# Experts of a routed layer: row gathers that skip empty slots, and finished rows written by GpSimd scatters

## The chip, the core and the metric

The kernel runs on one core of a Trainium2 chip. The core has five engines with queues of their own: TensorE (PE; its weight loads stand as PEld), VectorE (DVE), ScalarE (ACT), GpSimd (POOL) and SyncE (SP), and 16 DMA engines that serve all queues. The metric is the device time of one execution in microseconds, as a median of runs.

## The reference

Two blocks of a transformer on 512 tokens of width 1024. What matters is the mixture of experts at the end of the first block: 32 experts, each token goes to 4.

```
logits = hf @ router_w + router_b
top_val, top_idx = lax.top_k(logits, TOP_K)            # TOP_K = 4, 512 tokens
gate = softmax(top_val)
...
def expert_block(args):
    e, toks, wts = args
    u = hf[toks] @ w1[e] + b1[e]                       # w1[e]: 1024 x 2048
    g_, lin = u[:, :D_FF], u[:, D_FF:]
    g_ = jnp.minimum(g_, SWIGLU_LIMIT)
    lin = jnp.clip(lin, -SWIGLU_LIMIT, SWIGLU_LIMIT)
    y = ((lin + 1.0) * g_ * sigmoid(SWIGLU_ALPHA * g_)) @ w2[e] + b2[e]
    return y * wts[:, None]
...
out = segment_sum(y.reshape(R, D), row_tok, num_segments=T)
```

Everything is float32. The attention of two kinds ahead of the experts, and the second block behind them, are not touched but for one transfer.

## The kernel before

**Stages.** The program goes through stages with a barrier of all engines between them: norm and projections, attention (`attention`, to about 387 us of the profile), output projection and routing (`output_and_route`, to 480), the experts (`expert_blocks`, to 1554), `combine_and_norm`, and the second block.

**Blocks.** Each expert's tokens are the rows of one block; the row's slot in the block is its rank among the expert's tokens, so a block's real rows are its first ones. Experts are sorted by their count and laid out so that even blocks (and block 31) hold up to 128 rows and the other odd blocks up to 64: 17 blocks of 128 slots and 15 of 64. Rows past that go to overflow blocks (up to 15, blocks 32 to 46), which run only if there are any; in this profile there are none. A slot that has no row names token 0.

**Row traffic.** `output_and_route` writes the normed tokens to the DRAM tensor `h_dram` (h_rows in the profile) and builds `slots`, a token number for each slot of each block. In the experts GpSimd copies a block's column of `slots` into `col` (L1745) and gathers the rows of `h_dram` into `xg` by an indirect DMA (L1748), 128 or 64 rows of 4 KB. `xg` is single, so `next_rows(b)` waits until PE has transposed the block before (`x_turn`). A finished block is moved by ACT from PSUM into the SBUF tile `y` (L2030 for 128 rows, L2022 for 64) and stored by ACT's own DMA queue into `y_dram` (y_rows) as one contiguous piece (L2032, L2024); the next copy into `y` waits for `stored`. `combine_and_norm` gathers four rows of `y_dram` for each token.

**Weights.** Each expert has 12 chunks of 1024 KB. SP loads them into a ring of 8 slots (L1228) when PE has used a slot, ACT rounds a chunk into `w_hi` (L1997), DVE makes the rest `w_lo` by a subtraction (L2149), and PE multiplies with both. ACT's order is written by hand in `to_small(i)` and `from_small(i)`: 12 roundings, with the moves of rows in between. In `to_small` the odd block's `y` is copied after the fifth rounding (`few_rows_out`) and the even block's after the twelfth (`rows_out`).

**Zeros.** So that no row of `y_dram` that is never written holds garbage, the attention's SP fills the 15 overflow blocks with zeros (L932, last in SP's list for that stage), and `output_and_route` copies rows of x into the unused upper 64 slots of the odd blocks (L1306).

## Time and profile before

| | us |
|---|---|
| median of 3 runs | 3497.16 (3491.63 to 3498.02) |
| the profiled execution | 3498.6 |
| its span, first to last instruction | 3496.5 |
| experts, first chunk of the stage to the last store | about 480 to 1554 |

The page shows what each engine did over the whole span and in 40 slices of 87.4 us each. The experts fill slices 6 to 18. Shares of the whole span are means over stages with different limits; for this change the stage's own windows and waits are to be read.

### The profile page before, as it was taken

To read this page: it belongs to the slowest core of one execution; us is meant where nothing else is said; L and a number is where in the kernel's file an instruction comes from. 1 tells how busy PE (TensorE), PEld (TensorE's weight loads), DVE (VectorE), ACT (ScalarE), POOL (GpSimd) and SP (SyncE) were. 2 spreads that over 40 slices of the span, in tenths; PEclk is the share of its full clock that TensorE was granted. 3 is DMA by queue.
4 is the path that set the end of the run, shared out by engine and by line. 5 is a ranking of instruction groups with operands and counts; after the bars stand their busy time and mean duration, and the time that the engine had idled before them with its cause. 6 is when DMAs were issued, how large, how long until landed. Compare 5 with 4: busy or idle time off the path is not lost. (4 is left out here: it accounts for less than half of the span.)

```text
span 3496.5 us, 38713 instructions
## 1 busy us (share of the span) xinstructions
PE 3183.6 (91%) x13402; PEld 2163.4 (62%) x13402; DVE 2868.0 (82%) x4755; ACT 1432.8 (41%) x1763; POOL 714.8 (20%) x724
## 2 busy tenths in 40 slices
PE   7999989999999999999999999888888888888876
PEld 5878767777777777766788788543444434344422
DVE  6867689999999999967995645788888788888886
ACT  3235448888888888853233632111111111111110
POOL 0000001000000000010000200344444444444443
PEclk9999999999999999999999999999999999999999
DMA  7422279999999999974234025999999999999998
GB/s 264 168 85 103 75 261 393 407 407 403 406 405 401 406 403 403 410 273 138 95 98 133 13 97 199 391 421 417 421 412 415 413 407 421 418 417 410 414 421 344
DMA packets 251798, 1100.57 MB, mean 315 GB/s; under 512 B 21208, under 2 KB 30832, under 8 KB 185840
## 3 DMA queue, kind: packets, MB, share of 16 engines
q1 hardware_dynamic: 166221, 523.62, 39.3%
q0 software_dynamic: 79680, 558.14, 39.0%
q10 hardware_dynamic: 5760, 17.04, 1.2%
q8 instruction: 78, 1.28, 0.1%
q14 instruction: 59, 0.48, 0.0%
HBM read 1069.64 MB, written 33.03 MB: 315 GB/s over the span
## 5 line engine op out<-in xcount | busy, mean ns | idle before, releaser
L2149 DVE TENSOR_TENSOR moe_w_lo<-ring,moe_w_hi 128x2048 fp32r<-128x2048 f32 x384 | 860.7, 2282 | 27.9 <-ACT moe_w_hi L1997 26.5
L1997 ACT ACTIVATE moe_w_hi<-ring 128x2048 fp32r<-128x2048 f32 x380 | 721.6, 1916 | 163.7 <-DMA ring<-in_exp_w 149.0
L2938 PE MATMUL last_banks<-last_rows_b,ring 128*128 128x512 f32 x1024 | 504.4, 640 | 126.0 <-DVE ring L3138 125.8
L2938 PE MATMUL last_banks<-last_rows_a,ring 128*128 128x512 f32 x1024 | 476.7, 609 | 85.3 <-DVE ring L3138 84.9
L3030 ACT ACTIVATE last_gelu<-last_dot 128x2 f32<-128x2 f32 (+1 forms) x257 | 52.3, 203 | 1116.1 <-DVE last_dot L3135 1116.0
L2938 PEld LDWEIGHTS last_banks<-last_rows_b,ring 128*128 128x128 f32 x1024 | 198.8, 203 | 405.6 <-issue 211.2
L2938 PEld LDWEIGHTS last_banks<-last_rows_a,ring 128*128 128x128 f32 x1024 | 188.5, 193 | 327.8 <-issue 198.4
L2817 POOL DMA_INDIRECT last_rows_a<-in_peer_uv,last_ids x256 | 282.3, 1103 | 507.3 <-PE last_banks L2938 329.8
L2817 POOL DMA_INDIRECT last_rows_b<-in_peer_uv,last_ids x256 | 290.4, 1134 | 383.6 <-PE last_banks L2938 363.5
L3138 DVE TENSOR_SCALAR ring<-consts_sb,last_gelu,last_gates 128x128 f32<-128x128 f32 x512 | 162.0, 387 | 78.7 <-ACT last_gelu L3030 77.8
L1745 POOL COPY moe_col<-slots 128x1 uint32 (+1 forms) x30 | 35.7, 1191 | 861.3 <-PE moe_tp L1793 477.0
L3135 DVE CUSTOM_DVE_ANT_0 last_rows_b<-last_rows_b,ring 128x1024 f32<-128x1024 f32 x128 | 155.3, 1224 | 50.0 <-DMA last_rows_b<-in_peer_uv,last_ids 47.5
L3135 DVE CUSTOM_DVE_ANT_0 last_rows_b<-last_rows_b,last_h 128x1024 f32<-128x1024 f32 x128 | 154.5, 1223 | 37.0 <-DMA last_rows_b<-in_peer_uv,last_ids 34.0
L3135 DVE CUSTOM_DVE_ANT_0 last_rows_a<-last_rows_a,ring 128x1024 f32<-128x1024 f32 x128 | 154.0, 1221 | 35.8 <-DMA last_rows_a<-in_peer_uv,last_ids 34.7
L3135 DVE CUSTOM_DVE_ANT_0 last_rows_a<-last_rows_a,last_h 128x1024 f32<-128x1024 f32 x128 | 153.4, 1221 | 30.0 <-DMA last_rows_a<-in_peer_uv,last_ids 28.6
L2565 DVE SCALAR_TENSOR_TENSOR conv_rows<-glu,conv_taps,conv_rows 128x512 f32<-128x512 f32 x240 | 160.8, 741 | 0.5
L260 DVE TENSOR_TENSOR mix_lo<-ring,mix_hi 128x2048 fp32r<-128x2048 f32 (+1 forms) x48 | 107.2, 2245 | 49.4 <-ACT mix_hi L251 49.1
L251 ACT ACTIVATE mix_hi<-ring 128x2048 fp32r<-128x2048 f32 (+1 forms) x48 | 90.0, 1882 | 116.9 <-DMA ring<-in_w_in 50.9
L307 PE MATMUL conv_acc<-mix_hi,ht_hi 128*128 128x512 f32 x320 | 126.3, 395 | 0.0
L309 PE MATMUL conv_acc<-mix_hi,ht_lo 128*128 128x512 f32 x320 | 125.6, 393 | 0.0
L308 PE MATMUL conv_acc<-mix_lo,ht_hi 128*128 128x512 f32 x320 | 124.9, 390 | 0.0
L1083 DVE COPY spare<-att_pt 128x128 f32<-128x128 f32 (+3 forms) x160 | 78.2, 489 | 44.4 <-PE att_pt L975 40.8
(599 smaller groups left out, 6345.9 us busy)
## 6 DMA issues: line engine op xcount, KB each, us to landing
ring<-in_exp_w SPq DMA_DIRECT2D x384, 1024.0 KB, 11.5
ring<-in_w_in SPq DMA_DIRECT2D x38, 1024.0 KB, 5.4
ring<-in_ada_w SPq DMA_DIRECT2D x12, 1024.0 KB, 13.1
z<-in_ada_w SPq DMA_DIRECT2D x12, 1024.0 KB, 7.2
y_rows<-moe_y ACTq DMA_DIRECT2D x17, 512.0 KB, 6.7
ring<-in_w_out SPq DMA_DIRECT2D x8, 1024.0 KB, 5.0
y_rows<-spare SPq DMA_DIRECT2D x1, 7680.0 KB, 25.2
gate_rows<-conv_held ACTq DMA_DIRECT2D x4, 1024.0 KB, 8.2
```

What stands on the lines that cost most here:

```text
L251: self.env.nc.scalar.activation(self.hi[:, m % RAW, 0:n], self.raw[:, i % RAW, 0:n], ACT.Copy).then_inc(self.hi_done, 1)
L260: self.env.nc.vector.tensor_tensor(self.lo[:, i % RAW, 0:n], self.raw[:, i % RAW, 0:n], self.hi[:, m % RAW, 0:n].bitcast(F32), ALU.subtrac ...
L307: nc.tensor.matmul(out, lhs[0], rhs[0], start=start, stop=False)
L308: nc.tensor.matmul(out, lhs[0], rhs[1], start=False, stop=False)
L309: return nc.tensor.matmul(out, lhs[1], rhs[0], start=False, stop=stop)
L1997: nc.scalar.activation(w_hi[:, slot, :], env.ring[:, slot, :], ACT.Copy).then_inc(hi_done, 1)
L2149: nc.vector.tensor_tensor(w_lo[:, slot, :], env.ring[:, slot, :], w_hi[:, slot, :].bitcast(F32), ALU.subtract).then_inc(lo_done, 1)
L2565: ins = nc.vector.scalar_tensor_tensor(conv[:, n, :], glu[:, n, tap:tap + S], taps[:, n, tap:tap + 1], conv[:, n, :], ALU.mult, ALU.add)
L2817: nc.gpsimd.indirect_dma_start(slot(n), None, d["peer_uv"], bass.IndirectOffsetOnAxis(ids[:, u % 4, s:s + 1], 0)).then_inc(gathered[n % SL ...
L2938: last = nc.tensor.matmul(sums(t)[:, q, :], diag[:, n % SL], slot(n)[:, D + q * W:D + (q + 1) * W], start=first, stop=final)
L3135: nc.vector.tensor_tensor_reduce(left, left, h(t), 1.0, 0.0, ALU.mult, ALU.add, dot[:, n % SL:n % SL + 1]).then_inc(dotted, 1)
L3138: nc.vector.tensor_scalar(diag[:, n % SL], ident, act_out[:, n % SL:n % SL + 1], gates[:, u % 4, n % K:n % K + 1], ALU.mult, ALU.mult).the ...
```

## The change

Four things change.

- `slots` of an empty slot becomes a number past the end (`NO_ROW`), and the gathers get a bounds check that leaves such rows out. To tell an empty slot, the routing's count by block and slot uses t + 1 in place of t for the four token tiles, so that zero means empty.
- A second table `out_at` holds, for each block and slot, the row of `y_dram` to write, or `NO_ROW`. GpSimd copies its column into `out_col` and scatters `y` into `y_dram` by an indirect DMA with a bounds check. ACT's DMA issues and their waits are gone; ACT still copies PSUM into `y`, and still waits for `stored` before the next copy.
- GpSimd's order in the experts becomes gather, scatter, gather, scatter: `next_rows(b)` is followed by `rows_out(b - 3)`.
- `y_dram` is zeroed as a whole (47 blocks and not 15) in the attention, and the copies of x into unused slots go away.

```diff
-    attention(env, "att1", (z, z, z), heads, fill=y_dram[N_EXP * P:], ...)
+    attention(env, "att1", (z, z, z), heads, fill=y_dram, ...)
...
-            unused = m["y_dram"][0:N_EXP * P, :].rearrange("(g f r) n -> f g r n", f=4, r=HALF)[3]
-            some_rows = d["x"].rearrange("(g r) n -> g r n", r=HALF)
-            for g0, g1 in ((0, 8), (8, N_EXP // 2 - 1)):
-                sp.dma_start(unused[g0:g1], some_rows[0:g1 - g0]).then_inc(filled, 16)
...
-            sp.wait_ge(filled, 32)
...
-                chain.also(nc.vector.tensor_scalar(own, own, float(t), None, ALU.mult))
+                chain.also(nc.vector.tensor_scalar(own, own, float(t + 1), None, ALU.mult))
...
-            chain(nc.vector.tensor_copy(rows_lo[:], rows_ps[:, 0:NB]))
+            chain(nc.vector.tensor_scalar(empty[:], rows_ps[:, NB:2 * NB], 0.5, NO_ROW, ALU.is_lt, ALU.mult))
+            chain(nc.vector.tensor_scalar(rows_lo[:], iota[:, 0:NB], float(P), env.const("tok")[:, 0:1], ALU.mult, ALU.add))
+            chain(nc.vector.tensor_tensor(m["out_at"][:], rows_lo[:], empty[:], ALU.add))
+            chain(nc.vector.scalar_tensor_tensor(rows_lo[:], rows_ps[:, 0:NB], -float(P), empty[:], ALU.add, ALU.add))
             chain(nc.vector.scalar_tensor_tensor(m["slots"][:], rows_ps[:, NB:2 * NB], float(P), rows_lo[:], ALU.mult, ALU.add))
 
+NO_ROW = float(MAX_BLOCKS * P + 2 * S)
...
-                nc.gpsimd.indirect_dma_start(xg[0:rows], None, h_dram, bass.IndirectOffsetOnAxis(col[0:rows, 0:1], 0)).then_inc(gathered, 16)
+                nc.gpsimd.indirect_dma_start(xg[0:rows], None, h_dram, bass.IndirectOffsetOnAxis(col[0:rows, 0:1], 0),
+                                               bounds_check=S - 1, oob_is_err=False).then_inc(gathered, 16)
+
+            def rows_out(b, rows=P):
+                pool.wait_ge(y_moved, b + 2)
+                pool.sem_inc(tick, 1)
+                nc.gpsimd.tensor_copy(out_col[:], out_at[:, span(b, 1)]).then_inc(out_ready, 1)
+                pool.wait_ge(out_ready, b + 1)
+                pool.sem_inc(tick, 1)
+                nc.gpsimd.indirect_dma_start(y_dram, bass.IndirectOffsetOnAxis(out_col[0:rows, 0:1], 0), y[0:rows], None,
+                                             bounds_check=MAX_BLOCKS * P - 1, oob_is_err=False).then_inc(stored, 16)
...
-            with pool.Fori(0, (N_EXP - 4) // 2) as i2:
-                next_rows(i2 * 2 + 2, P)
-                next_rows(i2 * 2 + 3, HALF)
+            next_rows(2, P)
+            next_rows(3, HALF)
+            rows_out(0)
+            with pool.Fori(0, (N_EXP - 6) // 2) as i2:
+                next_rows(i2 * 2 + 4, P)
+                rows_out(i2 * 2 + 1, HALF)
+                next_rows(i2 * 2 + 5, HALF)
+                rows_out(i2 * 2 + 2)
             next_rows(N_EXP - 2, P)
+            rows_out(N_EXP - 5, HALF)
             next_rows(N_EXP - 1, P)
+            rows_out(N_EXP - 4)
+            rows_out(N_EXP - 3, HALF)
+            rows_out(N_EXP - 2)
+            rows_out(N_EXP - 1)
...
             def few_rows_out(b, n_small):
                 act.wait_ge(y_done, n_small + 1)
                 nc.scalar.activation(y[0:HALF], flat(yp, HALF), ACT.Copy).then_inc(y_moved, 1)
-                act.wait_ge(y_moved, b + 2)
-                act.dma_start(y_dram[span(b * P, HALF), :], y[0:HALF]).then_inc(stored, 16)
...
             def rows_out(b, chunks):
                 act.wait_ge(used, chunks)
-                act.wait_ge(stored, b * 16 + 16)
+                if not isinstance(b, int) or b > 0:
+                    act.wait_ge(stored, b * 16)
                 nc.scalar.activation(y[:], yp[:].rearrange("p q n -> p (q n)"), ACT.Copy).then_inc(y_moved, 1)
-                act.wait_ge(y_moved, b + 2)
-                act.dma_start(y_dram[span(b * P, P), :], y[:]).then_inc(stored, 16)
```

On GpSimd, the loop over pairs of blocks in the experts, before (moe_col is `col`, moe_xg the gathered rows, h_rows the tokens in DRAM):

```order
L1745 COPY moe_col<-slots 128x1
L1746 REGISTER_ALU
L1748 DMA moe_xg<-h_rows,moe_col 128x1024
L1751 REGISTER_ALU
L1753 REGISTER_ALU
L1745 ISA
L1745 COPY moe_col<-slots 128x1
L1746 REGISTER_ALU
L1748 DMA moe_xg<-h_rows,moe_col 64x1024
```

and now (moe_y is the finished block's tile, moe_out_col the column of rows to write, y_rows the target in DRAM):

```order
L1748 DMA moe_xg<-h_rows,moe_col 128x1024
L1753 REGISTER_ALU
L1755 ISA
L1755 COPY moe_out_col<-out_at 128x1
L1756 REGISTER_ALU
L1758 DMA y_rows<-moe_y,moe_out_col 6016x1024
L1762 REGISTER_ALU
L1764 REGISTER_ALU
L1745 ISA
L1745 COPY moe_col<-slots 128x1
L1746 REGISTER_ALU
L1748 DMA moe_xg<-h_rows,moe_col 64x1024
```

A scatter of the odd block now stands between the two gathers, and one of the even block behind the second.

On ACT, the end of the same loop from the copy of the odd block's rows, before:

```order
L2022 ACTIVATE moe_y<-moe_yp 64x1024
L2024 ISA
L2024 DMA y_rows<-moe_y 64x1024
L1997 ACTIVATE moe_w_hi<-ring 128x2048 x2
...
L2030 ACTIVATE moe_y<-moe_yp 128x1024
L2032 ISA
L2032 DMA y_rows<-moe_y 128x1024
```

and now:

```order
L2045 ACTIVATE moe_y<-moe_yp 64x1024
L2020 ACTIVATE moe_w_hi<-ring 128x2048 x2
...
L2051 REGISTER_ALU
L2052 ACTIVATE moe_y<-moe_yp 128x1024
```

The two DMA issues have left ACT's queue; the copies stand where they stood.

## Rows read from the trace of the kernel before

**Rows 1.** The page: busy time by engine, and DMA share in 40 slices.

```profile
PE 3183.6 (91%) x13402; PEld 2163.4 (62%) x13402; DVE 2868.0 (82%) x4755; ACT 1432.8 (41%) x1763; POOL 714.8 (20%) x724
...
DMA  7422279999999999974234025999999999999998
```

**Rows 2.** Windows: stretch, busy us of each engine, granted clock, DMA share, GB/s.

```profile
600.00:1400.00 800.00, 766.15 (x3461) 593.41 (x3460) 777.26 (x461) 656.78 (x446) 64.75 (x48) 1.00 1.03 405
```

**Rows 3.** Waits from 600 to 1400: us in total, times, longest.

```profile
ACT moe_w_hi L1997 <- DMA ring<-in_exp_w: 121.3, 153, 2.0
...
DVE moe_w_lo L2149 <- ACT moe_w_hi L1997: 20.9, 28, 1.5
```

**Rows 4.** Timeline of ACT: start, duration, instruction, idle time before it.

```profile
815.53 1.91 ACT L1997 ACTIVATE moe_w_hi<-ring 128x2048 fp32r<-128x2048 f32 x1 [0.65 <-DMA ring<-in_exp_w]
818.09 1.91 ACT L1997 ACTIVATE moe_w_hi<-ring 128x2048 fp32r<-128x2048 f32 x1 [0.65 <-DMA ring<-in_exp_w]
...
830.89 1.92 ACT L1997 ACTIVATE moe_w_hi<-ring 128x2048 fp32r<-128x2048 f32 x1 [0.63 <-DMA ring<-in_exp_w]
834.73 1.92 ACT L1997 ACTIVATE moe_w_hi<-ring 128x2048 fp32r<-128x2048 f32 x1 [1.92 <-DMA ring<-in_exp_w]
```

**Rows 5.** Windows: a 128-row gather lands (first), 64-row gathers land (others).

```profile
831.00:834.00 3.00, 3.00 (x14) 2.45 (x13) 3.00 (x2) 1.80 (x1) 0.00 (x0) 1.00 1.02 408
860.00:863.00 3.00, 3.00 (x15) 2.43 (x14) 3.00 (x2) 1.83 (x2) 0.00 (x0) 1.00 1.03 296
926.00:929.00 3.00, 3.00 (x15) 2.44 (x14) 3.00 (x2) 2.49 (x2) 0.00 (x0) 1.00 1.03 306
793.00:796.00 3.00, 3.00 (x14) 2.44 (x13) 3.00 (x3) 2.47 (x3) 0.00 (x0) 1.00 1.04 328
```

**Rows 6.** Window: the store of 128 rows is under way.

```profile
869.00:872.00 3.00, 2.79 (x13) 1.96 (x12) 3.00 (x2) 1.38 (x2) 0.00 (x0) 1.00 1.03 423
```

**Rows 7.** Timeline of GpSimd.

```profile
523.59 4.62 POOL L1745 COPY moe_col<-slots 128x1 uint32 x1 [25.41 <-PE moe_tp L1785]
...
824.06 1.91 POOL L1745 COPY moe_col<-slots 128x1 uint32 x1 [33.37 <-PE moe_tp L1793]
826.76 0.97 POOL L1748 DMA_INDIRECT moe_xg<-h_rows,moe_col  x1 [0.79 <-POOL moe_col L1745]
...
853.38 0.22 POOL L1745 COPY moe_col<-slots 128x1 uint32 x1 [25.65 <-PE moe_tp L1785]
854.39 2.29 POOL L1748 DMA_INDIRECT moe_xg<-h_rows,moe_col  x1 [0.78 <-POOL moe_col L1745]
...
890.29 1.91 POOL L1745 COPY moe_col<-slots 128x1 uint32 x1 [33.61 <-PE moe_tp L1793]
```

**Rows 8.** Timeline of ACT: copies of finished rows into y.

```profile
845.31 1.01 ACT L2022 ACTIVATE moe_y<-moe_yp 64x1024 f32<-64x1024 f32 x1
...
863.82 1.01 ACT L2030 ACTIVATE moe_y<-moe_yp 128x1024 f32<-128x1024 f32 x1
```

**Rows 9.** The page, DMA issues: KB each, median us from issue to landing.

```profile
ring<-in_exp_w SPq DMA_DIRECT2D x384, 1024.0 KB, 11.5
...
y_rows<-moe_y ACTq DMA_DIRECT2D x15, 256.0 KB, 5.9
```

**Rows 10.** Timeline of DVE: the router's last instruction.

```profile
478.39 0.21 DVE L1650 SCALAR_TENSOR_TENSOR slots<-out_acc,out_rows_lo 128x47 uint32<-128x47 f32 x1
```

**Rows 11.** Timeline of ACT and of GpSimd: the last store, the first combining gather.

```profile
1551.74 0.35 ACTq L2032 DMA_DIRECT2D y_rows<-moe_y  x1
...
1556.16 1.07 POOL L2296 DMA_INDIRECT got_rows<-y_rows,dest  x1 [104.04 <-POOLq L189]
```

**Rows 12.** Timeline of SP, and SP's wait for the zeros.

```profile
271.03 1.12 SPq L932 DMA_DIRECT2D y_rows<-spare  x1
386.92 0.38 SPq L1298 DMA_DIRECT2D z<-in_ln_g  x1
...
SPq L892 <- DMA y_rows<-spare: 24.1, 1, 24.1
```

More of the change, by code:

```diff
@@ L1177, in dve_between @@
             pieces.split_part(dve, splits.index(g) % 4)
-    attention(env, "att1", (z, z, z), heads, fill=y_dram[N_EXP * P:], loads=loads, act_between=act_between, dve_between=dve_between)
+    attention(env, "att1", (z, z, z), heads, fill=y_dram, loads=loads, act_between=act_between, dve_between=dve_between)
 def first_mixer(env, mod, y_dram, blocks):
@@ L1271, in output_and_route @@
         destf = sb("destf", [P, N]); blk = sb("blk", [P, N], U32); slot = sb("slot", [P, N], U32)
-        blkf = sb("blkf", [P, N]); slotf = sb("slotf", [P, N]); rows_lo = sb("rows_lo", [P, NB])
+        blkf = sb("blkf", [P, N]); slotf = sb("slotf", [P, N]); rows_lo = sb("rows_lo", [P, NB]); empty = sb("empty", [P, NB])
         acc = ps("acc", [P, 4, W])
@@ L1284, in output_and_route @@
             "eps_set", "copied", "chain"))
-        lifted, filled, first_ok, first_rows, compared, ordered, at_ok, at_done, numbered, x_turn, x_hi, row_names = (sem(n) for n in (
-            "lifted", "filled", "first_ok", "first_rows", "compared", "ordered", "at_ok", "at_done", "numbered", "x_turn", "x_hi", "row_names"))
+        lifted, first_ok, first_rows, compared, ordered, at_ok, at_done, numbered, x_turn, x_hi, row_names = (sem(n) for n in (
+            "lifted", "first_ok", "first_rows", "compared", "ordered", "at_ok", "at_done", "numbered", "x_turn", "x_hi", "row_names"))
         first_xg, first_col = gather_place(nc, "out1", m["rows_at"])
@@ L1657, in gather_place, with expert_blocks @@
     return nc.alloc_sbuf_tensor_at(f"{name}_xg", [P, D], F32, offset=at), nc.alloc_sbuf_tensor_at(f"{name}_col", [P, 1], U32, offset=at + 4 * D)
-def expert_blocks(env, slots, expert_at, over_expert, n_over, row_pick, parts, h_dram, y_dram, landed, rows_at, col_ready, gathered, hi_done, lo_done, w_hi, w_lo, bend, first_x_lo, first_xt):
+def expert_blocks(env, slots, out_at, expert_at, over_expert, n_over, row_pick, parts, h_dram, y_dram, landed, rows_at, col_ready, gathered, hi_done, lo_done, w_hi, w_lo, bend, first_x_lo, first_xt):
     nc, d = env.nc, env.d
@@ L1775, in _ @@
                     gather(o + N_EXP)
+                    rows_out(o + N_EXP)
             pool.sem_inc(tick, 1)
@@ L2022, in few_rows_out @@
                 nc.scalar.activation(y[0:HALF], flat(yp, HALF), ACT.Copy).then_inc(y_moved, 1)
-                act.wait_ge(y_moved, b + 2)
-                act.dma_start(y_dram[span(b * P, HALF), :], y[0:HALF]).then_inc(stored, 16)
             def rows_out(b, chunks):
                 act.wait_ge(used, chunks)
-                act.wait_ge(stored, b * 16 + 16)
+                if not isinstance(b, int) or b > 0:
+                    act.wait_ge(stored, b * 16)
                 nc.scalar.activation(y[:], yp[:].rearrange("p q n -> p (q n)"), ACT.Copy).then_inc(y_moved, 1)
-                act.wait_ge(y_moved, b + 2)
-                act.dma_start(y_dram[span(b * P, P), :], y[:]).then_inc(stored, 16)
             def to_small(i, eights, n_small, first=False):
@@ L2087, in _ @@
             act.sem_inc(y_moved, 1)
-            act.sem_inc(stored, 16)
             act.sem_inc(x_hi, 2)
@@ L2116, in _ @@
                     rows_out(b, o * 12 + MAIN_CHUNKS + 12)
-            act.wait_ge(stored, n * (16 * MAX_OVER) + (N_EXP + 1) * 16)
+            act.wait_ge(stored, n * (16 * MAX_OVER) + N_EXP * 16)
             act.sem_inc(tick, 1)
@@ L3282, in blocks @@
                     "gate": sb("gate", [P, NT, TOP_K]), "dest": sb("dest", [P, NT * TOP_K], U32),
-                    "slots": sb("slots", [P, MAX_BLOCKS], U32), "over_expert": sb("over_expert", [P, MAX_OVER], I32),
+                    "slots": sb("slots", [P, MAX_BLOCKS], U32), "out_at": sb("out_at", [P, MAX_BLOCKS], U32), "over_expert": sb("over_expert", [P, MAX_OVER], I32),
                     "expert_at": sb("expert_at", [P, N_EXP], I32), "bend": sb("bend", [P, N_EXP]), "first_x_lo": sem("first_x_lo"), "first_xt": [nc.alloc_sbuf_tensor_at(f"moe_xt_{n}_a", [P, KC, P], F32R, offset=rows_at + 4 * (D + 8 + i * KC * P)) for i, n in enumerate(("hi", "lo"))], "n_over": sb("n_over", [P, 1], I32), "row_pick": sb("row_pick", [P, MAX_BLOCKS]),
@@ L3294, in build @@
             held.close()
-            expert_blocks(env, m["slots"], m["expert_at"], m["over_expert"], m["n_over"], m["row_pick"], m["parts"], m["h_dram"], y_dram, m["landed"],
+            expert_blocks(env, m["slots"], m["out_at"], m["expert_at"], m["over_expert"], m["n_over"], m["row_pick"], m["parts"], m["h_dram"], y_dram, m["landed"],
                           m["rows_at"], m["col_ready"], m["gathered"], m["hi_done"], m["lo_done"], m["w_hi"], m["w_lo"], m["bend"], m["first_x_lo"], m["first_xt"])
```

4 lines of the change are left out of this document (3 added, 1 removed).

## The prediction

> **What bounds the kernel now.** I read the page's busy shares and its forty slices first [rows 1]. No engine owns the program: PE is 91% busy and DVE 82%, and the DMA line reads 9 in slices 7 to 17 and again at the end. The change lies in the first of these stretches, the experts, so I read that stretch alone. Between 600 and 1400 us [rows 2] the 16 DMA engines are busy all the time (share 1.03) and move 405 GB/s, DVE works 777.3 of 800 us and PE 766.2. Both are nearly full, so the waits must say who sets the pace. ACT waits 121.3 us there for expert weights to land, and DVE waits 20.9 us for ACT's rounding of them [rows 3]; nothing else holds DVE. In ACT's own timeline [rows 4] two roundings that waited for a landing start at 815.53 and 818.09: one 1024 KB chunk lands every 2.56 us, which is 1.0486 MB / 2.56 us = 410 GB/s. So the stage is set by the DMA engines, and DVE is the next limit, 22.7 us per 800 behind.
>
> One pair of blocks (one of 128 rows, one of 64) takes 66.2 us, from the column copy at 824.06 to the one at 890.29 on GpSimd [rows 7]. Its 24 chunks take 24 x 2.56 = 61.4 us. The remaining **4.8 us are the row traffic** that the change touches: a gather of 128 rows, a gather of 64, a store of 128, a store of 64. From 600 to 1400 us that is 12 pairs, over all experts about 15.
>
> **What each row transfer costs.** This decides the case.
> - The gather of 128 rows (512 KB): the chunk after it is rounded at 834.73 and not at 833.45 [rows 4], 3.84 us after the one before, thus 1.28 us more. By bytes at 410 GB/s it would be 1.28 us. The rate while its rows land is 408 GB/s [rows 5].
> - The gather of 64 rows (256 KB): by bytes 0.64 us. But while its rows land the rate falls to 296, 306 and 328 GB/s, mean 310, at a full DMA share [rows 5]. Three microseconds at 310 where 408 is usual lose 3 x 98 / 408 = 0.72 us, so it costs 1.36 us. It costs **as much as the gather of twice the rows**.
> - The stores: 423 GB/s beside one of 128 rows [rows 6], no loss of rate, so by bytes 1.28 us and 0.64 us.
> - Sum 1.28 + 1.36 + 1.28 + 0.64 = 4.56 of the 4.8 us.
>
> **What skipping saves.** 17 blocks have 128 slots and 15 have 64, 3136 in all; 512 tokens with 4 choices fill 2048. A third of the slots are empty, always the upper ones of a block, because a row's slot is its rank. If the time fell with the rows, a pair would save 0.347 x 4.8 = 1.67 us, and 15 pairs **25 us**; DVE would just allow it (22.7 us per 800 are 28 us over some 990). This is one bound. The other is nothing, and I take that one. The reason is the pair of gathers: if only the number of rows counted, 64 rows would cost half of 128. They don't, so slots 64 to 127 go by ways to SBUF and by DMA engines that the lower 64 slots don't load; with them left out, the lower 64 are what the slowest engine has to move, as before. A chunk of weights needs all its engines, and the loads are what the pace hangs on. A mean expert fills 64 slots, so in the 128-slot blocks nearly all that is skipped is the upper half, and in the 64-slot blocks little is skipped. For the stores the trace doesn't show which engine carries which slot; bounds 0 and 0.347 x 1.92 = 0.67 us a pair, 10 us in all; I take 0 here too, by the gathers' rows.
>
> The Trainium skill ("DMA: Bandwidth & Descriptors", "The descriptor swizzle") says that in a transfer to 128 partitions engines 0 to 7 serve partitions 0 to 63 and engines 8 to 15 the rest. By that rule a block's empty upper half frees engines 8 to 15 alone and the stage gains 0 us, against 25 us by the plain sum of bytes. The two rates of the gathers agree with it; no row names an engine.
>
> **Scatters in place of ACT's stores.** ACT loses 32 DMA issues (0.35 us for the last [rows 11]). ACT waits for landings anyway, so this gives 0. On GpSimd a finished block now needs a copy of its column and an indirect DMA. The copies took 0.22, 1.91 and once 4.62 us, the long ones since GpSimd stood behind DVE's back-to-back subtractions; then 0.79 us pass, then the indirect DMA takes 0.97 or 2.29 us [rows 7]. A scatter is thus issued 2.0 to 7.7 us after the rows are there, 3.3 to 3.7 us in the pair shown.
>
> Who waits for that: ACT's copy of the next even block needs the odd block's rows stored. The odd rows are in y at 846.33, the next copy into y starts at 863.82 [rows 8]: a window of 17.5 us. Issue 3.7 + landing 5.9 us (the store of 64 rows now [rows 9]) = 9.6: it fits. Behind the waiting GpSimd stand the gathers. The gather issued at 854.39 comes after a scatter that GpSimd is done with by 851 or so, the one at 824 after one done by 870 in the pair before; both keep their times. A copy that slips in between two subtractions can hold DVE for its own 0.22 us at most: 31 more copies are 0 to 7 us, and DVE's 28 us of idle time cover them.
>
> The Trainium skill ("SBUF — State Buffer", "Who interferes with whom") says that a DVE instruction with two SBUF inputs and a GpSimd instruction that reads SBUF shut each other out, which speaks against work on GpSimd here. The copy of 4.62 us agrees. By that rule each new scatter may be late by one or two subtractions of 2.28 us, which the window still holds.
>
> **The head.** The router's tail on DVE has two operations of 0.21 us after the last matmul; now there are five. It is the last work before the experts (0.21 us, 0.24 from start to start [rows 10]): 3 x 0.24 = **+0.7 us**.
>
> **The tail.** The last store is issued at 1551.74 in 0.35 us, and the combining gathers start at 1556.16 [rows 11]. Now: a copy while DVE rests 0.22, 0.79, indirect DMA 0.97 [rows 7], less 0.35 = +1.6 us. The landing is unknown for a scatter; it lies within the 4.1 us that the rows leave after the issue, so a quarter more or less is 1 us. I take **+2.0 us**.
>
> **The zeros.** 15 blocks (7680 KB) held SP for 24.1 us [rows 12]; 47 blocks take 75.5 us, from 271.0 to 348. SP has nothing else until 386.9. Hidden, with 38 us to spare; only below 213 GB/s, against 326 now, would the barrier wait. The removed copies of x into unused slots (L1306) stand in front of nothing that waits: 0.
>
> Sum: 3498.6 us for the profiled execution + 0.7 + 2.0 = 3501.3. That execution is 1.4 us above the median of 3497.2, so the forecast for the median is **3500 us**.
>
> **Rivals.**
> 1. *The skipped rows do relieve every DMA engine.* For it: the stage is DMA-bound and rows cost by bytes in three of the four transfers. Against it: the 64-row gather. In full 3500 - 25 = 3475; if only the stores gain 3500 - 10 = 3490; halfway 3487. Chance 0.22 of more than 7 us.
> 2. *The scatter of the odd block comes too late,* slower. ACT would then stand before its copy into y, and with it the rounding of weights. It decides from 17.5 us on. If GpSimd is held for two subtractions (4.62 + 0.79 + 2.29 = 7.7) and the scatter lands like a chunk (11.5 us [rows 9]), it is 1.7 us late. Each us costs up to 1 us in 15 pairs: 1 us late gives 3515, 1.7 us 3525. Chance 0.17.
> 3. *Nothing is skipped on the wire:* an empty slot still costs a packet. The time is the forecast's, 3500, and the bytes of GpSimd's queue tell it apart. Chance 0.08.
> 4. *As forecast*, within 0.2% of before: 0.53; with the third 0.61.
>
> 0.2% (7 us) is about what a measurement of this kernel can tell from no change. So: faster 0.22, same 0.61, slower 0.17. The range: below, most of the first rival but its full size, 3480; above, the second at 1 us, 3513.
>
> **What would show it.** Right: a pair still takes 66 us; GpSimd's queue loses about 4 MB of gathers and gains about 8 MB of scatters, ACT's queue loses its 13 MB of stores; the DMA share falls below 1.03 at an unchanged pace; the rate during the small gather stays low; the combine starts some 2 us later behind the last expert. Rival 1: pairs of 64.5 to 65.5 us, chunks after a 128-slot gather 3.3 us apart and not 3.84. Rival 2: a wait of ACT's L2052 copy for a DMA. The forecast fails if the slowest engine in a transfer is one of those that the upper slots use, or if a bounds-checked indirect DMA costs GpSimd much more than 2.3 us.

## The result, and the profile after

The changed kernel takes **3515.3 us** (median of 11 runs, 3509.1 to 3530.5) against 3498.0 for the kernel before beside it: ratio 1.0055, 95% interval 1.0045 to 1.0066. The forecast was 3500 with a range of 3480 to 3513. It is slower, by 0.5%, and outside the range.

The profiled execution takes 3516.6 us, its span 3514.8, which is 18.3 more than before. The page, busy time by engine and DMA share in slices, then packets and queues:

```profile
PE 3191.9 (91%) x13402; PEld 2171.3 (62%) x13402; DVE 2873.8 (82%) x4758; ACT 1432.9 (41%) x1763; POOL 833.3 (24%) x788
...
DMA  7427179999999999964234024999999999999998
...
DMA packets 255820, 1104.74 MB, mean 314 GB/s; under 512 B 23314, under 2 KB 32938, under 8 KB 189921
...
q0 software_dynamic: 83328, 562.31, 39.1%
q10 hardware_dynamic: 2112, 4.19, 0.3%
```

GpSimd has 118 us more work than in [rows 1], and slice 4 of the DMA line shows the zeros. ACT's queue q10 carried 17.04 MB before and carries 4.19. Packets under 512 B are 2106 more than before (21208), about two for each of the 1088 empty slots, one for its gather and one for its scatter. a3_no_skip (below), which moves every slot by the same route, has the same 255820 packets in all, but 21193 small ones and 8.7 MB more: a skipped slot still costs a packet, but no 4 KB.

The same stretch and waits as [rows 2, 3], and ACT's copies of blocks 2 and 28 into y:

```profile
600.00:1400.00 800.00, 765.61 (x3440) 594.53 (x3439) 775.02 (x458) 653.99 (x445) 151.98 (x97) 0.99 1.02 394
...
ACT moe_w_hi L2020 <- DMA ring<-in_exp_w: 143.1, 175, 2.3
...
DVE moe_w_lo L2168 <- ACT moe_w_hi L2020: 22.6, 60, 1.8
...
598.78 1.03 ACT L2052 ACTIVATE moe_y<-moe_yp 128x1024 f32<-128x1024 f32 x1 [0.78 <-PE moe_yp L1857]
...
1465.23 1.00 ACT L2052 ACTIVATE moe_y<-moe_yp 128x1024 f32<-128x1024 f32 x1
```

The same two copies in the kernel before:

```profile
598.57 1.01 ACT L2030 ACTIVATE moe_y<-moe_yp 128x1024 f32<-128x1024 f32 x1
...
1458.01 1.01 ACT L2030 ACTIVATE moe_y<-moe_yp 128x1024 f32<-128x1024 f32 x1
```

The DMA engines are still busy all the time (1.02), but move 394 and not 405 GB/s. That is some 9 MB less in 800 us, and ACT waits 22 us longer for it. From block 2 to block 28 (13 pairs) it takes 866.4 us; before it was 1458.01 - 598.57 = 859.4. This is the first loss: **+7.0 us**, where I had put 0.

One pair in ACT's timeline, beside [rows 4]:

```profile
832.74 1.92 ACT L2020 ACTIVATE moe_w_hi<-ring 128x2048 fp32r<-128x2048 f32 x1 [0.58 <-DMA ring<-in_exp_w]
836.54 1.92 ACT L2020 ACTIVATE moe_w_hi<-ring 128x2048 fp32r<-128x2048 f32 x1 [1.88 <-DMA ring<-in_exp_w]
839.07 1.91 ACT L2020 ACTIVATE moe_w_hi<-ring 128x2048 fp32r<-128x2048 f32 x1 [0.60 <-DMA ring<-in_exp_w]
...
842.38 1.92 ACT L2020 ACTIVATE moe_w_hi<-ring 128x2048 fp32r<-128x2048 f32 x1 [0.49 <-DMA ring<-in_exp_w]
844.95 1.92 ACT L2020 ACTIVATE moe_w_hi<-ring 128x2048 fp32r<-128x2048 f32 x1 [0.65 <-DMA ring<-in_exp_w]
```

In the kernel before, the third chunk behind the late one at 834.73:

```profile
842.40 1.92 ACT L1997 ACTIVATE moe_w_hi<-ring 128x2048 fp32r<-128x2048 f32 x1 [0.48 <-DMA ring<-in_exp_w]
```

The chunk beside the gather of 128 slots still comes 3.80 us after its forerunner (before 3.84): the skipped rows bought nothing there. And 839.07 to 842.38 is another 3.31 us, 0.75 late, where before the three chunks behind the late one took 2.56 us each (7.67 us).

The tail: GpSimd's last scatter and first combining gather, PE there, and two windows with the granted clock (the number behind the five engines):

```profile
1559.97 0.18 POOL L1755 COPY moe_out_col<-out_at 128x1 uint32<-128x1 uint32 x1 [7.91 <-ACT moe_y L2052]
1561.01 0.98 POOL L1758 DMA_INDIRECT y_rows<-moe_y,moe_out_col  x1 [0.86 <-POOL moe_out_col L1755]
1568.88 0.98 POOL L2315 DMA_INDIRECT got_rows<-y_rows,dest  x1 [6.90 <-POOLq L189]
...
1568.23 3.75 PE L314 MATMUL norm_sums<-consts_sb 128*128 128x512 f32 x4 [6.06 <-PEq L189]
...
1568.00:1575.00 7.00, 6.09 (x10) 2.58 (x11) 2.16 (x9) 3.99 (x13) 4.75 (x5) 0.50 0.63 195
1575.00:1590.00 15.00, 15.00 (x28) 5.67 (x27) 3.61 (x3) 1.70 (x3) 10.30 (x11) 0.80 1.00 387
```

In the kernel before, ACT's last copy, PE there, and two windows:

```profile
1550.69 1.02 ACT L2030 ACTIVATE moe_y<-moe_yp 128x1024 f32<-128x1024 f32 x1 [11.47 <-PE moe_yp L1834]
...
1555.50 1.96 PE L314 MATMUL norm_sums<-consts_sb 128*128 128x512 f32 x4 [1.41 <-PEq L189]
...
1554.00:1560.00 6.00, 3.91 (x12) 1.72 (x12) 2.13 (x9) 3.80 (x12) 2.95 (x3) 1.00 0.40 115
1560.00:1575.00 15.00, 15.00 (x36) 6.03 (x35) 5.18 (x5) 3.33 (x7) 11.62 (x12) 1.00 1.02 374
```

ACT's last copy starts at 1558.78, so the combining gathers start 10.1 us behind it; before it was 5.5 (1550.69, and 1556.16 in [rows 11]). GpSimd's own queue (L189, the barrier of the stages) holds them 6.9 us behind its last indirect DMA. Its rows landed 3.2 us after their issue, those of ACT's store before 2.6 us, so the landing makes 0.6 us of the difference. PE stands idle for 6.06 us, and then its granted clock is 0.50, the 1.2 GHz level, for 7 us and 0.80 for 15 more, where it was 1.00 before. From the first combining gather to the end of the last `norm_turned` matmul it takes 48.9 and not 43.1 us. So 18.3 = 7.0 (blocks 2 to 28) + 0.9 (last blocks) + **4.6** (tail) + **5.8** (combine). Everything else cancels.

### The profile page after: what moved, and what is told of

The parts are those of the page before. It is cut to its first block and busy times, and to the rows that moved or that the text cites. A ratio compares the mean times of both kernels' runs of the same rounds, so it can differ in the third digit from the quotient of the medians.

```text
span 3514.8 us, 38854 instructions
## 1 busy us (share of the span) xinstructions
PE 3191.9 (91%) x13402; PEld 2171.3 (62%) x13402; DVE 2873.8 (82%) x4758; ACT 1432.9 (41%) x1763; POOL 833.3 (24%) x788
## 2 busy tenths in 40 slices
DMA packets 255820, 1104.74 MB, mean 314 GB/s; under 512 B 23314, under 2 KB 32938, under 8 KB 189921
## 3 DMA queue, kind: packets, MB, share of 16 engines
q10 hardware_dynamic: 2112, 4.19, 0.3%
## 5 line engine op out<-in xcount | busy, mean ns | idle before, releaser
L1755 POOL COPY moe_out_col<-out_at 128x1 uint32 (+1 forms) x32 | 49.6, 1551 | 466.0 <-ACT moe_y L2045 322.2
L1745 POOL COPY moe_col<-slots 128x1 uint32 (+1 forms) x30 | 56.4, 1878 | 353.4 <-PE moe_tp L1816 276.1
## 6 DMA issues: line engine op xcount, KB each, us to landing
y_rows<-spare SPq DMA_DIRECT2D x1, 24064.0 KB, 65.6
```

## The experiments

Each was timed against the kernel before on the same chip. The columns are stretches of the profiled executions, from the starts and ends in their timelines: ACT's copy of block 2 to that of block 28; last copy to first combining gather; from there to the last `norm_turned`; from there to the first matmul of the second attention; from that attention's last matmul to the first gather of the last stage. Stretches of the same code differ by some us from execution to execution: the start up to SP's filling took 268.0 to 276.4 us. Each row of the table is one execution, the ratio a median of 5 to 12. Those of a3 (3498.3 us, median 3506.4) and c1 (3489.8, median 3498.6) were the fastest of their kernels, and c3's lay 5.8 us below its median. A single row is therefore good to about 5 us, and conclusions below rest on groups of rows.

| kernel | ratio (interval) | 2 to 28 | tail | combine | to attention | behind it |
|---|---|---|---|---|---|---|
| before | | 859.4 | 5.5 | 43.1 | 327.5 | 132.3 |
| after | 1.0055 (1.0045, 1.0066) | 866.4 | 10.1 | 48.9 | 327.5 | 132.3 |
| a1_tail_act | 1.0024 (1.0015, 1.0032) | 870.7 | 5.4 | 43.2 | 327.0 | 132.3 |
| a2_busy | 1.0040 (1.0028, 1.0051) | 872.6 | 10.1 | 43.2 | 327.0 | 132.3 |
| a3_no_skip | 1.0027 (1.0015, 1.0039) | 857.3 | 10.1 | 46.9 | 327.0 | 132.1 |
| a4_gather_skip | 0.9993 (0.9983, 1.0003) | 859.5 | 5.5 | 43.1 | 327.0 | 132.5 |
| b1_scatter_skip | 1.0034 (1.0021, 1.0047) | 870.3 | 5.4 | 44.9 | 327.0 | 133.6 |
| b2_route_only | 1.0010 (1.0000, 1.0020) | 862.6 | 5.4 | 44.9 | 327.5 | 133.5 |
| b3_gather_skip_route | 1.0034 (1.0022, 1.0047) | 869.6 | 5.4 | 43.2 | 325.5 | 132.3 |
| b4_spread (rows missing) | 1.0009 (1.0000, 1.0018) | 846.4 | 7.2 | 44.8 | 331.1 | 134.3 |
| c1_spread | 1.0012 (1.0000, 1.0023) | 848.8 | 7.3 | 44.8 | 329.6 | 134.0 |
| c2_spread_no_skip | 1.0037 (1.0023, 1.0050) | 857.4 | 7.3 | 49.0 | 331.1 | 134.3 |
| c3_skip_big | 1.0040 (1.0027, 1.0052) | 868.4 | 5.4 | 43.2 | 325.5 | 132.3 |
| c4_skip_small | 1.0009 (1.0000, 1.0018) | 861.8 | 5.4 | 44.9 | 327.0 | 132.0 |
| d1_spread_aligned | **0.9972** (0.9962, 0.9983) | 853.1 | 7.6 | 43.2 | 320.9 | 131.1 |
| d2_two_columns | 1.0010 (0.9999, 1.0021) | 858.5 | 5.5 | 43.1 | 331.6 | 134.3 |
| d3_order | 1.0453 (1.0439, 1.0468) | 1006.5 | 5.4 | 43.2 | 325.5 | 132.3 |
| d4_spread_order | 1.0445 (1.0431, 1.0460) | 1004.6 | 7.6 | 43.2 | 322.5 | 131.4 |
| e1_sixteen_columns | 0.9980 (0.9971, 0.9990) | 857.5 | 5.5 | 43.1 | 322.8 | 131.1 |
| e2_old_places | 1.0020 (1.0007, 1.0032) | 867.7 | 7.6 | 44.8 | 322.5 | 131.4 |

### The tail: GpSimd's barrier and PE's clock

**a1_tail_act**

```diff
-            rows_out(N_EXP - 2)
-            rows_out(N_EXP - 1)
...
-                rows_out(i, at(i, 12))
-                rows_out(b, at(b, 4))
+                for last, chunks in ((i, at(i, 12)), (b, at(b, 4))):
+                    ...
+                    rows_out(last, chunks, last)
+                    act.wait_ge(y_moved, last + 2)
+                    act.dma_start(y_dram[span(last * P, P), :], y[:]).then_inc(kept, 16)
```

> The changed kernel, but blocks 30 and 31, the last two, are stored by ACT's own DMA queue as before the change; GpSimd scatters blocks 0 to 29. Theory T (the tail): GpSimd's barrier stands some 5 us behind its last indirect DMA, and the 6 us in which PE is idle there cost it its clock in the combine. Then the time from the last copy into y to the first combining gather falls from 10.1 to 5.5 us, PE's idle time ahead of its norm_sums matmuls from 6.1 to 1.4 us, the stage from the first combining gather to the last norm_turned matmul from 18.5 to 12.7 us: 3515.3 - 4.6 - 5.8 = 3505 us. Rival T2 (the combine is slow because its gathers follow scatters or read rows that were written row by row): only the 4.6 us come back, 3511. Rival T3 (the wait is for the landing of the scatter, not for GpSimd): 3.2 us of landing become about 2, 3514.

**a2_busy**

```diff
-            keep_busy(nc, env, glu_ps[:, 0, :], 4)
+            keep_busy(nc, env, glu_ps[:, 0, :], 9)
```

> The changed kernel, but PE runs 9 and not 4 of the spare matmuls at the end of the experts (0.9 us each), so that it stays at work while it stands before the barrier. Theory T (the combine is slow by PE's clock alone, which falls in the 6 us of idle time): idle time ahead of norm_sums from 6.1 to 1.5 us, granted clock 1.00 in the 7 us behind it, the combine stage 12.7 and not 18.5 us, the gap from the last copy to the first combining gather still 10.1: 3515.3 - 5.8 = 3509.5 us. Rival T2 (slow gathers): no change, 3515.

First gather and PE's first matmuls of the combine in a1, then the same two in a2 with the window behind them:

```profile
1568.62 0.98 POOL L2324 DMA_INDIRECT got_rows<-y_rows,dest  x1 [35.24 <-POOLq L189]
...
1567.98 1.96 PE L314 MATMUL norm_sums<-consts_sb 128*128 128x512 f32 x4 [1.44 <-PEq L189]
```

```profile
1575.05 0.99 POOL L2315 DMA_INDIRECT got_rows<-y_rows,dest  x1 [6.90 <-POOLq L189]
...
1574.40 1.95 PE L314 MATMUL norm_sums<-consts_sb 128*128 128x512 f32 x4 [1.77 <-PEq L189]
...
1574.50:1581.50 7.00, 6.33 (x17) 2.57 (x18) 2.11 (x8) 5.57 (x15) 4.92 (x6) 1.00 0.69 222
```

Theory T holds in both parts. Without a scatter at the end the tail is 5.4 us, PE waits 1.44 and its four matmuls take 1.96 us. With the scatter, but PE kept at work, the tail stays 10.1 and the combine takes 43.2: the 5.8 us are the clock's alone. T2 and T3 fall. T3 said that the wait is for the landing; then the tail would have come down by 1.2 us, and it came down by 4.7. (The expectations put the combine at 18.5 and 12.7 us, which is not the stretch of the table; the difference, 5.8, is the same.) Both kernels ended above their forecasts, by 4 us; blocks 2 to 28 took 871 to 873 us in them, 4 to 6 more than in the changed kernel.

### The pace: which of the parts costs it

**a3_no_skip**

```diff
+            chain(nc.vector.tensor_copy(m["out_at"][:], rows_lo[:]))
+            chain(nc.vector.tensor_scalar(rows_lo[:], rows_ps[:, 0:NB], -float(P), None, ALU.add))
+            chain(nc.vector.scalar_tensor_tensor(rows_lo[:], rows_ps[:, NB:2 * NB], float(P), rows_lo[:], ALU.mult, ALU.add))
+            chain(nc.vector.tensor_scalar(m["slots"][:], rows_lo[:], 0.0, None, ALU.max))
```

> The changed kernel, but no slot is skipped: an empty slot names token 0 in the gathers as before the change, and the scatters write every row of y (128 or 64) to its own place. What stays is the route: GpSimd's scatters in place of ACT's stores, its order, and the filling with zeros. For the 7 us that blocks 2 to 28 lost (from ACT's copy of block 2 to that of block 28, 859.4 us before and 866.5 after the change): theory S (the skipping does it, since it makes the DMA engines uneven) expects 859.5 again and 3508 us. Rival R (the route does it: scatters in a queue of GpSimd's, its copies beside DVE) expects 866 or more, up to 25 us worse if the skipping did save bytes: 3515 to 3535. The tail stays as in the changed kernel for both.

**a4_gather_skip**: the kernel before with the changed `slots` and the gathers' `bounds_check=S - 1`.

> The kernel before, with one part of the change alone: the gathers of the experts skip empty slots (an empty slot's number is past the end). Stores, filling and the order stay as before; the rows of y in empty slots are computed from what the tile held. Theory S (skipping makes the DMA engines uneven and costs pace): the stretch from block 2 to block 28 grows from 859.4 by 3 to 7 us, 3501 to 3505. Rival R (the route alone costs it): 859.4 within 1 us, 3498.5. Rival G (skipped rows do relieve the engines): 859.4 less 3 to 13 us, 3486 to 3495.

Without any skip the scatters cost nothing (857.3), so the route by itself is innocent, as theory S expects; what a3 loses against the kernel before is the tail (4.6) and the combine (3.8). With ACT's stores the skip of the gathers costs nothing either, and gains nothing: rival G is out, and so is theory S, which expected 3 to 7 us more here. It takes a skip and the scatters.

**b1_scatter_skip**: a1_tail_act with the `slots` of a3. **b2_route_only**: that, and the `out_at` of a3. **b3_gather_skip_route**: a1_tail_act with the `out_at` of a3.

> The changed kernel with blocks 30 and 31 stored by ACT (as a1_tail_act, so that the tail is that of before), and of the two skips only that of the scatters: the gathers fetch token 0 for an empty slot again. Measured is the stretch from ACT's copy of block 2 to that of block 28: 859.4 us before, 866 to 873 with both skips, 857.3 with GpSimd's scatters and no skip, 859.5 with the gathers' skip alone. Theory S2 (skipping in the scatters costs it): 866 to 871, 3506 to 3510 us. Rival S1 (what counts is how far the engines of the upper slots run ahead, and that adds up from both skips): 859 to 863, between the ends, 3499 to 3503.

> The changed kernel without any skip and with blocks 30 and 31 stored by ACT: only GpSimd's scatters in place of ACT's stores for blocks 0 to 29 are left. If the route costs nothing and the tail was all that a3_no_skip lost: block 2 to block 28 in 857 to 858 us, the gap from the last copy to the combine 5.5, the combine stage 43.1 us: 3496 to 3498 us, at or just below the kernel before. Rival (scatters cost something that one execution of a3_no_skip hid): 3502 or more.

> The complement of b1_scatter_skip: scatters of all rows, gathers that skip, blocks 30 and 31 stored by ACT. Theory S2 (the scatters' skip costs it): block 2 to block 28 in 857 to 860 us, 3496 to 3500. Rival S1 (the engines' unevenness adds up from both skips): 859 to 863, as b1, 3499 to 3503.

b1 came out as S2 expects, b3 as neither, and b2 took 5 us more in this stretch than forecast (3499.7 in all and not 3496 to 3498). Beside scatters each skip by itself costs the whole, 870.3 and 869.6, and both together no more (866.4 to 872.6 in the four kernels that have both in the old places); without a skip it is 857.3 and 862.6. The 7 us from b2 to b3 are the gathers' skip and nothing else by their code; that two such kernels without a skip differ by 5 us is the measure of how far to trust them.

**c3_skip_big**

```diff
+            chain(nc.vector.memset(empty[:, 1:N_EXP - 2:2], 0.0))
```

**c4_skip_small**

```diff
+            chain(nc.vector.memset(empty[:, 0:N_EXP:2], 0.0))
+            chain(nc.vector.memset(empty[:, N_EXP - 1:NB], 0.0))
```

> The changed kernel in its own order, blocks 30 and 31 stored by ACT, with the skips (gather and scatter) only in the blocks of 128 slots; in those of 64 slots every slot is moved. Theory E (unevenness costs): the upper half of the big blocks is where nearly all is skipped, so block 2 to block 28 stays at 866 to 872 us as with all skips, 3505 to 3510 us. Rival (the cost comes from the blocks of 64 slots, whose gather lands slowest as it is): 857 to 863, 3497 to 3501.

> The complement of c3_skip_big: skips only in the blocks of 64 slots, which are four fifths full. Theory E: 857 to 864 us from block 2 to block 28, 3497 to 3502 us. Rival: 866 to 872, 3505 to 3510.

Skipping in the blocks of 128 slots, where it is the upper half that is empty, costs the time (868.4); in the blocks of 64 it costs little (861.8, within what kernels without skips take). By packets under 512 B, c3 has 1626 more than a3 and c4 368: the big blocks hold four fifths of the skips. So these two runs don't tell uneven skipping from much skipping; the next ones do.

### The places of the rows

**b4_spread** and **c1_spread** keep both skips and put the rows elsewhere. The rank r of a row (bits r6 to r0) goes to slot bits 6 to 0 = r3 r6 r2 r1 r0 r5 r4 in a block of 128, and r6 r3 r2 r1 r0 r5 r4 in one of 64. DVE compares with two rows of such ranks in place of 0 to 127, and `out_at` holds b x 128 + rank. The last two blocks are stored in four DMAs with the rows put back in order. b4 leaves out the first choices of the first 128 tokens in nearly all blocks (6% of the rows).

```diff
+def rank_at(q):
+    return (q & 64) | (q >> 2 & 8) | (q >> 2 & 7) | (q & 3) << 4
...
+                for to, row in ((of_slot, rank_row), (of_big, rank_big)):
+                    last = nc.vector.tensor_tensor(to[:, n0:n1], slotf[:, n0:n1]..., row[:]..., ALU.is_equal)
...
+            chain(nc.vector.tensor_tensor(m["out_at"][:], out_rows[:], empty[:], ALU.add))
```

y_dram keeps the order of ranks, since the scatter can write a row anywhere. Costs in the head: 16 x 2 more small matmuls and two compares, 2 to 3 us. Theory U (the engines of the lower slots set the pace, skipping frees the others alone, and makes them run ahead): now every engine moves a third fewer row packets, block 2 to block 28 falls from 859.4 by up to 13 x 1.7 = 22 us to 838 to 848, 3480 to 3490 us, faster than both kernels. Rival V (an indirect DMA with skipped rows is itself slow, whatever the engine): 866 to 871 as without the spreading, 3508 to 3512. Rival W (DVE is the next bound at once): 853 to 858, 3495 to 3499.

> b4_spread again (rows spread evenly over the slots, both skips, blocks 30 and 31 stored without GpSimd), with two mends: the matmuls that place the rows no longer drop the first choice of each token tile's entries, which was missing in b4 (some 6% of the rows), and the last two blocks are stored by two DMAs of ACT's and two of SP's rather than by four of ACT's. Theory U (evenly spread skips take row bytes from every DMA engine): block 2 to block 28 in 846 to 849 us against 859.4 before, the gap to the combine 6.0 to 6.5 us, and at the end 3487 to 3497 us, at or below the kernel before. Rival (what b4 saved was due to its missing rows): 850 to 860, 3500 to 3508.

**c2_spread_no_skip**: c1 with `slots` and `out_at` as in a3, the new places kept.

> c1_spread without any skip: the rows lie in the spread order, but an empty slot is gathered (token 0) and scattered as well. Control for the order by itself. Theory U: block 2 to block 28 in 857 to 863 us, as the two kernels without skips in the old order (857.3 and 862.6), thus the skips are worth 10 to 15 us once they are even. Rival (the order itself helps, whatever is skipped): 846 to 852.

c1's stretch of [rows 2], its copies of blocks 2 and 28, and c2's window:

```profile
600.00:1400.00 800.00, 769.70 (x3505) 607.49 (x3504) 784.98 (x467) 664.66 (x452) 233.67 (x98) 0.99 1.02 401
...
599.71 1.03 ACT L2081 ACTIVATE moe_y<-moe_yp 128x1024 f32<-128x1024 f32 x1 [0.66 <-PE moe_yp L1884]
...
1448.53 1.03 ACT L2081 ACTIVATE moe_y<-moe_yp 128x1024 f32<-128x1024 f32 x1
```

```profile
600.00:1400.00 800.00, 765.08 (x3476) 600.96 (x3475) 780.46 (x462) 659.59 (x449) 176.95 (x98) 0.99 1.03 405
```

Theory U's stretch comes out in both, 846.4 and 848.8. The same skipped rows (a1 and c1 have 1994 small packets more than their kernels without skips, b2 and c2) cost 7 to 13 us in the old places and save 9 us in the new ones (848.8 against 857.4 for c2), and the places alone do nothing. d1, below, has c1's experts and takes 853.1, so the saving is 4 to 9 us. By groups of rows: 857.3 to 862.6 in the eight kernels that don't lose (before, a3, a4, b2, c2, c4, d2, e1), 866.4 to 872.6 in the seven that skip the upper slots of the big blocks with scatters, 846.4 to 853.1 in the three that spread and skip. In the 800 us DVE does 467 instructions, 458 after the change, and is busy 785 us. b4's further 2 us may be its missing rows.

Yet c1 as a whole was no faster than the kernel before: 3498.6 us, where 3487 to 3497 was forecast, and b4 3499.0 where 3480 to 3490 was. The table doesn't give the reason in full, since c1's row is its fastest execution, 8.8 us below its median. In that row the tail is 1.9 us longer and the combine 1.7, and in the last two columns the three spread kernels take 329.6 to 331.1 and 134.0 to 134.3 us, those above them 325.5 to 327.5 and 132.0 to 133.6.

### Where the gain was given back

**d1_spread_aligned**: c1 with the two new columns of constants padded to 16, and `keep_busy(..., 7)`. **d2_two_columns** and **e1_sixteen_columns**: the kernel before and nothing but

```diff
+        "unused": np.zeros((P, 2)),
```

and the same with 16. **e2_old_places**: a1_tail_act with the 16 columns and `keep_busy(..., 7)`.

> c1_spread with two changes outside the experts: its two new columns of constants are padded to 16 (64 bytes a partition and not 8), and PE runs 7 spare matmuls and not 4 behind the last expert. In all spread kernels the stretch behind the combine was 2 to 5 us longer (329.6 to 331.1 and not 325.5 to 327.5 us up to the second attention, 134.0 to 134.3 and not 132 to 133 behind it). Theory M (the 8 bytes moved every later tile off its alignment): both stretches come back, 4 to 5 us, and the combine stage is 43 us and not 45 to 49, so 3489 to 3493 us, faster than the kernel before. Rival (the slots' order itself lengthens them): no change there, 3496 to 3499.

> The kernel before with two columns of constants that nothing reads, so that every tile allocated behind them stands 8 bytes further. Theory M: up to the second attention 329.5 to 331 us and not 327.5, behind it 134 and not 132.3, 3500 to 3502 us in all. Rival: as the kernel before, 3496.

> The kernel before with 16 columns of constants that nothing reads (64 bytes a partition), nothing else. d1_spread_aligned, which has this shift too, took 320.9 us from the combine to the second attention and not 327.5, and 131.1 and not 132.3 behind it; two columns (8 bytes) had made them 331.6 and 134.3. Theory M (these stretches hang on where tiles stand): 321 and 131 us here as well, 3489 us. Rival (the shift of 64 bytes is neutral and d1 gained by its order of rows): 327.5 and 132.3, 3496 to 3497.

> d1_spread_aligned without the spreading: rows in their old places, both skips, blocks 30 and 31 stored by ACT, 16 unused columns, 7 spare matmuls. The difference from d1 is the spreading by itself, at the kernel's whole time. Theory U: block 2 to block 28 in 866 to 872 us against 853.1 in d1, the rest as in d1 or 2 us shorter at the tail: 3499 to 3506 us, 12 to 18 above d1's 3487.6. Rival (the gain in the experts is given back elsewhere): within 5 us of d1.

A group of 320 matmuls between the combine and the second attention (busy us, mean ns of one), in the kernel before, d2, e1 and d1:

```profile
L307 PE MATMUL conv_acc<-mix_hi,ht_hi 128*128 128x512 f32 x320 | 126.3, 395 | 0.0
```

```profile
L308 PE MATMUL conv_acc<-mix_hi,ht_hi 128*128 128x512 f32 x320 | 127.4, 398 | 0.0
```

```profile
L308 PE MATMUL conv_acc<-mix_hi,ht_hi 128*128 128x512 f32 x320 | 125.5, 392 | 0.0
```

```profile
L316 PE MATMUL conv_acc<-mix_hi,ht_hi 128*128 128x512 f32 x320 | 125.5, 392 | 0.0
```

Theory M holds both ways in these stretches. Eight bytes more a partition make every such matmul 3 ns longer (c1 has 398 too) and the two stretches 4.1 and 2.0 us; 64 bytes make it 3 ns shorter and them 4.7 and 1.2 us (e2 has 392 too). For the whole kernel only the gain of e1 is clear of the noise; d2's interval still holds 1. I had not foreseen that 64 bytes would beat the kernel before; the forecast was that they restore it. Why this address is better the profile doesn't tell.

So d1 beats both kernels, 0.9972, 9 us below the kernel before, but unused columns alone give 0.9980. The spreading is judged by d1 against e2, which differ in it and in what it brings along (the head's extra compares and matmuls, the last two blocks' stores in four parts): 0.9972 to 1.0020, some **17 us**. Blocks 2 to 28 show 14.5 of them, which is the lost cost of the uneven skips and the saving together; 3.2 more stand in the combine and in the stretch to the attention, which lie outside the experts. The 7 spare matmuls have a price too: e2's tail is 7.6 us and a1's, with 4 of them, 5.4. What the whole change is worth done so is d1 against e1: 0.0008, within the intervals.

### The order on GpSimd

**d3_order** (on a1_tail_act) and **d4_spread_order** (on d1):

```diff
                 next_rows(i2 * 2 + 4, P)
-                rows_out(i2 * 2 + 1, HALF)
                 next_rows(i2 * 2 + 5, HALF)
+                rows_out(i2 * 2 + 1, HALF)
                 rows_out(i2 * 2 + 2)
```

> a1_tail_act (both skips, old order of rows, blocks 30 and 31 stored by ACT), with one exchange in GpSimd's loop: the gather of the block of 64 comes before the scatter of the block of 64, not behind it. With ACT's stores the store of 64 rows was issued 7.6 us before that gather, with the scatters it is 5.6 us before, and the chunk of weights that lands beside the gather is 1.0 to 2.9 us late when rows are skipped, 0.8 to 1.0 with ACT's stores. Theory N (the scatter that lands just ahead of the gather, in the same queue, makes the skips cost 8 to 12 us): block 2 to block 28 comes to 857 to 862 us, 3497 to 3502. Rival (the unevenness costs it wherever the scatter stands): 866 to 873, 3505 to 3511.

> d1_spread_aligned with the exchange of d3_order. With rows spread evenly theory N expects a small gain, 845 to 848 us from block 2 to block 28; the rival none, 848 to 850. In all 3487 to 3493 us.

ACT's wait from 600 to 1400 us, GpSimd and ACT in one pair of d3, and in the next pair the copy of the odd block's rows into y and GpSimd's next copy:

```profile
ACT moe_y L2054 <- DMA y_rows<-moe_y,moe_out_col: 131.9, 10, 13.7
...
829.02 4.50 POOL L1745 COPY moe_col<-slots 128x1 uint32 x1 [25.49 <-PE moe_tp L1808]
834.39 0.98 POOL L1748 DMA_INDIRECT moe_xg<-h_rows,moe_col  x1 [0.88 <-POOL moe_col L1745]
835.37 7.08 POOL L1755 COPY moe_out_col<-out_at 128x1 uint32 x1
843.33 0.94 POOL L1758 DMA_INDIRECT y_rows<-moe_y,moe_out_col  x1 [0.88 <-POOL moe_out_col L1755]
...
851.09 1.02 ACT L2054 ACTIVATE moe_y<-moe_yp 128x1024 f32<-128x1024 f32 x1 [13.74 <-DMA y_rows<-moe_y,moe_out_col]
...
899.64 1.02 ACT L2045 ACTIVATE moe_y<-moe_yp 64x1024 f32<-64x1024 f32 x1
...
907.70 4.50 POOL L1745 COPY moe_col<-slots 128x1 uint32 x1 [25.49 <-PE moe_tp L1808]
```

The runs don't decide the question they were made for: 4.5% slower, and all of it is the second rival of the prediction come true. The odd block's rows are in y at 900.66, but GpSimd now stands in front of the gather and waits for PE until 907.70: 7.0 us. The gather with its copy takes 6.4 us more (829.02 to 835.37), and the scatter's column copy, beside DVE's subtractions, 7.08. ACT waits 13.2 us on average (131.9 in ten times, 13.7 at most) for the odd block's rows; blocks 2 to 28 take 136 us longer than in a1 and 151 longer than in d1.

## Why the prediction was wrong, point by point

- **What bounds the stage: right.** Chunks come every 2.5 to 2.6 us where nothing else is moved, in both kernels, and in c1, where rows cost less, DVE is next (785 of 800 us).
- **Skipping: the value was wrong, the reason borne out in part.** The step that failed is "the other is nothing, and I take that one". That upper slots load other ways and engines than lower ones fits the runs with scatters, though none shows an engine: in the old places the chunk beside the 128-slot gather keeps its 3.8 us, and in the new ones bytes count. But nothing was not the end of the range. Leaving the upper slots out cost 7.0 us in the profile of after, 7 to 13 in its relatives. I gave bounds of 0 and 25 us and none below zero, without a reason that excluded a loss.
- **The stores' skip** was put at 0 by the gathers' rows. Beside scatters and without the gathers' skip it does the same harm as that (b1).
- **Scatters in place of stores: right.** a3, b2 and c2 take 857 to 863 us with them. GpSimd's 87 us more of work in 800 hold nobody in the pair shown; a copy of 12.09 us was seen once, where the prediction's worst case was 4.62:

```profile
534.40 12.09 POOL L1755 COPY moe_out_col<-out_at 128x1 uint32<-128x1 uint32 x1 [4.03 <-ACT moe_y L2052]
```

- **The window of ACT's next copy: right.** No wait of ACT for a store is seen from 600 to 1400. The scatter is issued at 850.34, the next copy at 866.96. d3 and d4 show the price when it doesn't hold, 10 to 12 us a pair.
- **The head: +0.7, not contradicted.** `slots` is ready at 478.88 and not 478.60, but the start of the program alone differs by 1.0 us between the two profiles.
- **The zeros: right, hidden.** Issued at 272.0, landed 65.6 us later, 50 us before SP's next work.
- **The tail: the term was 2.0 and measured 4.6.** The instructions were as forecast: 0.18, 0.86 and 0.98 us. What failed is the limit "within the 4.1 us that the rows leave after the issue", for those rows knew GpSimd only with its last indirect DMA 104 us behind it [rows 11]. Now the barrier came right behind one, and held it 6.9 us: 2.8 more than the 4.1, beside 1.8 more for the instructions.
- **What hangs on the tail: not seen at all,** 5.8 us. A wait of PE is not over when it ends; its clock was the next cost.
- **Rivals.** None was it. The first had the sign wrong, the second didn't occur, the third is refuted by bytes: only the packet remains. The range failed for two unpriced terms on the slow side, 7 and 5.8 us, with 2.6 us more of the tail than forecast.

What stays open: by what way uneven skipping slows the loads, and why the gathers' skip does no harm beside ACT's stores (a4: 859.5) and costs 7 to 12 us beside scatters (b3: 869.6, against 862.6 in b2 and 857.3 in a3). That the places of the skipped slots decide between cost and saving is shown (a1, b2, c1, c2, and d1 against e2); that it goes by uneven load of DMA engines is the reading that led to the new places, and no run shows it. Why the barrier holds GpSimd so long behind an indirect DMA whose rows have landed stays open too. The exchange of order that should have told drowned in another wait.

## What to carry to other kernels

In this stage work left out paid only when it was spread: ask what carries the rows that are skipped, and price the loss as well as the gain. An indirect DMA as GpSimd's last act before a barrier cost all engines 4.6 us here, and PE its clock behind it (5.8 us); let another queue do the last one. Before two steps of an engine's order are exchanged, look at what the one put first waits for: its wait now stands before the other. Before a gain or loss of 0.2% is put down to a change, move the tiles by some bytes without it and see what that does.
